# Column strips of 32 at the state products of a state-space layer, and strips by token phase for two of its input units

## The reference, cut to what matters

```python
u, z = proj[..., :1024], proj[..., 1024:]            # proj = h @ w_in
ug = u.reshape(bsz, seq, 64 groups, 16 channels)
in = f * einsum('blgc,gpc->blgp', ug, b)             # complex, 64 states a group
s[t] = a * s[t-1] + in[t]                            # complex scan over tokens
y = real(einsum('blgp,gcp->blgc', s, c)) + d_skip * u
y = gelu(y)
y = y * sigmoid(y @ w_glu + b_glu) * silu(z)
return y @ w_out
```

## Time and profile before

| what | value |
|---|---|
| median of the timed runs | 1353.59 us |
| the profiled execution | 1355.93 us, span 1354.1 us |
| granted TensorE clock, mean | 0.999 |
| PE busy / PE weight loads | 1333.1 us (98%) / 1230.2 us (91%) |
| VectorE busy | 860.0 us (64%) |
| ScalarE busy | 715.9 us (53%) |
| DMA queue for weights | 234.92 MB, 52.6% of 16 engines |

### The profile page before, as it was taken

The page is one execution under the profiler, slowest core; times in us unless marked ns, Lnnn a source line. Parts: engine busy times, 40 slices in busy tenths (PEclk is TensorE's granted clock), DMA queues, the critical chain, the costliest instruction groups (busy, mean ns, idle before and its releaser), DMA issues.

```text
span 1354.1 us, 23214 instructions
## 1 busy us (share of the span) xinstructions
PE 1333.1 (98%) x10110; PEld 1230.2 (91%) x10110; DVE 860.0 (64%) x1003; ACT 715.9 (53%) x954; POOL 54.8 (4%) x70
## 2 busy tenths in 40 slices
PE   6998999999999999999999999999999999999998
PEld 6998889889999989998999998999989999899997
DVE  6999775756555577767645547555466858655553
ACT  5998566655444463375544445444465355544443
POOL 1002000000000003100000000000000500000000
PEclk9999999999999999999999999999999999999999
DMA  9116555455555564455655565556565546555552
GB/s 271 62 32 212 159 199 187 136 179 172 187 190 198 203 205 169 152 190 184 201 187 187 187 208 182 187 190 199 199 205 193 175 133 203 193 187 187 187 187 93
DMA packets 180297, 242.28 MB, mean 179 GB/s; under 512 B 7547, under 2 KB 144005, under 8 KB 180197
## 3 DMA queue, kind: packets, MB, share of 16 engines
q1 hardware_dynamic: 178260, 234.92, 52.6%
q0 software_dynamic: 1648, 5.67, 1.5%
q10 hardware_dynamic: 288, 0.22, 0.0%
HBM read 239.74 MB, written 1.05 MB: 178 GB/s over the span
## 4 chain that ended last, share of the span: by engine, by line
PE 89%; DVE 9%; issue 1%; DMA 1%; ACT 0%; DVEq 0%; ACTq 0%; POOLq 0%
PE P L415 87%; PE P L450 1%; DVE QQ L1761 1%; DMA G<-in_norm_g 1%; DVE YG L1740 0%; DVE WB L1751 0%; DVE QQ L1765 0%; DVE WL L1445 0%; DVE TMPC L1712 0%; DVE TMPC L1709 0%; DVE QQ L1752 0%; DVE X L1725 0%; DVE TMPD L1678 0%; DVE TMPD L1710 0%; DVE DB L1969 0%
## 5 line engine op out<-in xcount | busy, mean ns | idle before, releaser
L1445 DVE TENSOR_TENSOR WL<-RAW,WH 128x2048 fp32r<-128x2048 f32 x214 | 485.7, 2277 | 305.9 <-ACT WH L1013 304.7
L415 PE MATMUL P<-RH,WH 128*128 128x256 f32 x1856 | 516.8, 278 | 4.3 <-DVE RL L1448 3.0
L415 PE MATMUL P<-RL,WH 128*128 128x256 f32 x1856 | 513.8, 277 | 0.0
L415 PE MATMUL P<-RH,WL 128*128 128x256 f32 x1856 | 513.7, 277 | 0.0
L1013 ACT ACTIVATE WH<-RAW 128x2048 fp32r<-128x2048 f32 x214 | 406.4, 1903 | 194.1 <-DMA RAW<-in_ffn_w_down 82.5
L415 PEld LDWEIGHTS P<-RH,WH 128*128 128x128 f32 x1856 | 348.9, 188 | 6.8 <-DVE RL L1448 2.3
L415 PEld LDWEIGHTS P<-RL,WH 128*128 128x128 f32 x1856 | 348.6, 188 | 1.5
L415 PEld LDWEIGHTS P<-RH,WL 128*128 128x128 f32 x1856 | 348.9, 188 | 0.0
L415 PE MATMUL P<-WH,HLO 128*128 128x512 f32 x352 | 138.7, 394 | 0.0
L415 PE MATMUL P<-WL,HHI 128*128 128x512 f32 x352 | 138.1, 392 | 0.0
L415 PE MATMUL P<-WH,HHI 128*128 128x512 f32 x352 | 137.1, 389 | 0.0
(11 more groups left out here) (306 smaller groups left out, 1376.7 us busy)
## 6 DMA issues: line engine op xcount, KB each, us to landing
RAW<-in_ffn_w_gate SPq DMA_DIRECT2D x88, 512.0 KB, 4.3
RAW<-in_ffn_w_up SPq DMA_DIRECT2D x88, 512.0 KB, 5.7
RAW<-in_ffn_w_down SPq DMA_DIRECT2D x44, 1024.0 KB, 5.0
RAW<-in_w_in SPq DMA_DIRECT2D x36, 1024.0 KB, 5.2
RAW<-in_attn_w_in SPq DMA_DIRECT2D x16, 1024.0 KB, 5.3
RAW<-in_ssm_w_in SPq DMA_DIRECT2D x8, 1024.0 KB, 9.6
RAW<-in_w_out SPq DMA_DIRECT2D x8, 1024.0 KB, 5.1
RAW<-in_ssm_w_glu SPq DMA_DIRECT2D x4, 1024.0 KB, 6.9
```

The lines of the kernel that those rows point to most:

```text
L415: return nc.tensor.matmul(*a, **k)
L1445: V.tensor_tensor(WL[:, s, 0:width], RAW[:, s, 0:width], WH[:, s, 0:width].bitcast(f32), SUB).then_inc(sem["lo_split"], 1)
```

## The change

- Units 2 and 3 are no longer multiplied by `plain` but by the new `phased`: for each of the 8 blocks of 32 weight columns, each of 8 contraction tiles and each of 4 phases q one call with 32 stationary columns and 64 moving columns, every fourth token of `XN`, into partitions 32 q to 32 q + 31. The bank then has the layout of X4, and one copy of 128x512 replaces sixteen, on ScalarE for unit 2 and on VectorE for unit 3.
- `states_in` makes each call through `strips`: four calls with 32 stationary columns each, to the four 32-partition parts of the output, with the same moving tile.
- `states_out` goes over half band, phase i and q with strips of 32 columns (one phase of one j each), so that the output's partitions are channels and its columns are phase and chunk. The lifts on VectorE go, and `y_out` is one gelu of 128x512 per band, whose destination steps by four elements.
- ScalarE's split of unit 9 is now made ahead of the last band's gelu, not in the middle of it.

```diff
-LIFT = [4, 4, 2, 2]
+            def phased(u, bank):
+                w = RAW[:, slot_of(u), :].rearrange("p (k c) -> p k c", k=KT)
+                x = XN.rearrange("p k (c i) -> p k i c", i=CL)
+                eng.wait_ge(sem[loaded[slot_of(u)]], pe.next(loaded[slot_of(u)], 16))
+                free(bank)
+                for j in range(8):
+                    for k in range(KT):
+                        for q in range(4):
+                            last = mm(P[bank][32 * q:32 * q + 32, j * NCH:j * NCH + NCH], w[:, k, 32 * j:32 * j + 32],
+                                      x[:, k, CL - 1 - q, :], start=j == 0 and k == 0, stop=j == 7 and k == KT - 1, skip_group_check=True)
+                last.then_inc(sem["unit_used"], 1)
-                plain(cb, cb)
+                (plain if cb == 1 else phased)(cb, cb)
+            def strips(o, lh, rh):
+                for q in range(0, 128, 32):
+                    last = mm(o[q:q + 32], lh[:, q:q + 32], rh, start=True, stop=True, skip_group_check=True)
+                return last
-                        last = mm(PP[2 + b % 2][...], BT[:, ri, j, :], X4[:, j, :], start=True, stop=True)
+                        last = strips(PP[2 + b % 2][...], BT[:, ri, j, :], X4[:, j, :])
-                for jj in range(JB):
-                    j = JB * b + jj
-                    mm(own(jj), TZ[:, j, :], X4[:, j, :], start=jj == 0, stop=False, skip_group_check=True)
+                def own(m, q, i):
+                    c = m * T + i * NCH
+                    return P[Y_BANK[b]][32 * q:32 * q + 32, c:c + NCH]
+                for m in range(2):
+                    for i in range(CL):
+                        for q in range(4):
+                            j = JB * b + 4 * m + q
+                            mm(own(m, q, i), TZ[:, j, 32 * i:32 * i + 32], X4[:, j, :],
+                               start=m == 0 and i == 0, stop=False, skip_group_check=True)
-                        v = CP[:, ri, j, :, :].rearrange("p n c -> p (n c)")
-                        last = mm(own(jj), v, u[:, ri, jj, :], start=False, stop=ri == 1 and jj == JB - 1, skip_group_check=True)
+                for m in range(2):
+                    for i in range(CL):
+                        for ri in range(2):
+                            for q in range(4):
+                                jj = 4 * m + q
+                                last = mm(own(m, q, i), CP[:, ri, JB * b + jj, i, :], u[:, ri, jj, :], start=False,
+                                          stop=m == 1 and i == CL - 1 and ri == 1, skip_group_check=True)
-            for q in range(4):
-                for s in range(CL):
...
+            fn(X4[:, 16:24, :], P[2].rearrange("p (j c) -> p j c", c=NCH), ACT.Copy).then_inc(sem["x4_there_b"], 1)
...
+            V.tensor_copy(X4[:, 24:32, :], P[3].rearrange("p (j c) -> p j c", c=NCH)).then_inc(sem["x4_there_v"], 1)
...
+                dst = YG[:, 2 * b:2 * b + 2, :].rearrange("p m (c i) -> p m i c", i=CL)
+                src = P[Y_BANK[b]].rearrange("p (m i c) -> p m i c", m=2, i=CL)
+                fn(dst, src, ACT.Gelu_apprx_tanh).then_inc(sem["y_raw"], 1)
...
             for b in range(NB):
-                y_out(b, split_hi if b == NB - 1 else None)
+                if b == NB - 1:
+                    split_hi()
+                y_out(b)
                 y_high(b)
...
-            lift(NB - 2)
             split_lo()
             for b in range(NB):
-                if b == NB - 1:
-                    lift(b)
```

More of the change, by code:

```diff
@@ L264, in build @@
             q_made angle_in sines_there f_there small_there b_there cx_there b_turned c_turned bt_there c_there k_there lags_there lags_copied lags_full compact_there ub_cleared tz_there tz_cleared
-            frac_there table_there in_there in_read unrotated y_raw powers_there x4_there_a x4_there_b x4_there_v gain_d_there params_there c_powers b_summed c_summed c_spread y_lifted dec_cleared dec_there scanned x_again
+            frac_there table_there in_there in_read unrotated y_raw powers_there x4_there_a x4_there_b x4_there_v gain_d_there params_there c_powers b_summed c_summed c_spread dec_cleared dec_there scanned x_again
             glu_sig y_gated y_hi y_lo r_hi r_lo qk_squared qk_rms qk_scaled qk_roped qk_turned qk_there gains_in rope_there
@@ L570, in states_in @@
                         j = JB * b + jj
-                        last = mm(PP[2 + b % 2][:, ri * 512 + jj * NCH:ri * 512 + jj * NCH + NCH], BT[:, ri, j, :], X4[:, j, :],
-                                  start=True, stop=True)
+                        last = strips(PP[2 + b % 2][:, ri * 512 + jj * NCH:ri * 512 + jj * NCH + NCH], BT[:, ri, j, :], X4[:, j, :])
                 last.then_inc(sem["in_there"], 1)
@@ L584, in states_out @@
                 u = (UBA, UBB)[b // 2][:, b % 2]
-                def own(jj):
-                    return P[Y_BANK[b]][:, jj * NCH:jj * NCH + NCH]
-                for jj in range(JB):
-                    j = JB * b + jj
-                    mm(own(jj), TZ[:, j, :], X4[:, j, :], start=jj == 0, stop=False, skip_group_check=True)
+                def own(m, q, i):
[7 more added lines that the diff above has]
+                               start=m == 0 and i == 0, stop=False, skip_group_check=True)
                 if b == 0:
@@ L594, in states_out @@
                 eng.wait_ge(sem["unrotated"], b + 1)
-                for jj in range(JB):
-                    j = JB * b + jj
-                    for ri in range(2):
-                        v = CP[:, ri, j, :, :].rearrange("p n c -> p (n c)")
-                        last = mm(own(jj), v, u[:, ri, jj, :], start=False, stop=ri == 1 and jj == JB - 1, skip_group_check=True)
+                for m in range(2):
[5 more added lines that the diff above has]
+                                          stop=m == 1 and i == CL - 1 and ri == 1, skip_group_check=True)
                 last.then_inc(sem["y_summed"], 1)
@@ L1102, in _ @@
             eng.wait_ge(sem["unit_used"], 3)
-            for q in range(4):
-                for s in range(CL):
-                    dst = X4[32 * s:32 * s + 32].rearrange("p (m q) c -> p q m c", q=4)[:, q, 4:6, :]
-                    src = P[2][32 * q:32 * q + 32, :].rearrange("p (m c i) -> p i m c", m=2, i=CL)[:, CL - 1 - s]
-                    fn(dst, src, ACT.Copy).then_inc(sem["x4_there_b"] if q == 3 and s == CL - 1 else act.raised(), 1)
+            fn(X4[:, 16:24, :], P[2].rearrange("p (j c) -> p j c", c=NCH), ACT.Copy).then_inc(sem["x4_there_b"], 1)
             eng.wait_ge(sem["c_turned"], 1)
@@ L1158, in toeplitz, with y_out @@
                            ACT.Copy).then_inc(sem["tz_there"] if lag == CL - 1 else act.raised(), 1)
-            def y_out(b, between=None):
+            def y_out(b):
                 eng.wait_ge(sem["y_summed"], b + 1)
[L1163 to L1175, removed]
+                dst = YG[:, 2 * b:2 * b + 2, :].rearrange("p m (c i) -> p m i c", i=CL)
+                src = P[Y_BANK[b]].rearrange("p (m i c) -> p m i c", m=2, i=CL)
+                fn(dst, src, ACT.Gelu_apprx_tanh).then_inc(sem["y_raw"], 1)
             def y_high(b):
@@ L1731, in lags_back @@
                 V.tensor_copy(KTS[:, 0:4, :], P[2].rearrange("p (m l) -> p m l", m=4)).then_inc(sem["lags_full"], 1)
[L1733 to L1740, removed]
             def rows_of(i, b):
```

## The result

The changed kernel takes 1368.14 us (median of 4, 1367.49 to 1371.27) against 1354.05 us (median of 4 runs of the kernel before): 1.0106 of the time before, 95% interval 1.0094 to 1.0118. That is 14 us slower, where 9 us faster was forecast, and outside the range. The profiled execution took 1367.98 us.

The account below looks back on a forecast made before the run. Three about equally long chains (PE, DVE, ACT) in the first layer's state-space stage bound the gain: second gate unit 10.0 us earlier, less 1.4 for phased units, -8.6 us, median 1345.0 us; range 1340 to 1366.

Parts of the forecast that it names:

- The phased units: Units 2 and 3 on PE: 15 ns a record for stepped reads and instruction stream together, 7.7 us each, +1.4 us in all.
- all three chains: First layer's state-space stage: PE, DVE and ACT work of about equal length, all moved by longer phased units.
- P: Length of one phased unit (2 or 3) on PE; 7.0 us if the step is free, 7.7 taken, upper end 28.
- The formula: Start of the B transposes, and with it all three chains, moves by 2 x (P - 7.0) us.
- Rival 2: Units 2 and 3: the stepped read halves the streams, P = 13.9, net +3.8 us, 1357.4; chance 0.26.
- Rival 4: Instruction fetching, 20 ns a record by the reflection; its own forecast text is not given; counted as same, chance 0.10.
- A strip of 64 columns at 13.6 to 15 ns: State inputs and outputs: 13.6 ns a strip record, 128 records in 1.75 us in place of 3.6; phased units at 15.
- Rotations 3.4 us earlier for the copies removed: DVE: sixteen X4 copies become one, so the first rotation starts at 71.65 in place of 75.05 us.
- One gelu a band at 1.0 us: ACT: the small gelus become four of 128x512, taken at 1.0 us each, bounds 0.6 and 1.6.
- The tail: From PE's last state output at 113.3 us to the second gate unit at 120.6, in place of 120.2 to 130.61.
- The sum without the phased price: Forecast for e1: 10.0 us gain less 3.4 for the returned copies, 6.6 us, about 1347.5.
- rival 5: PE's new idle stretches halve the granted clock for strips and first gate unit, about +3 us; within the forecast's own spread.

Follow-up runs that it names:

- e4: e1 with `plain` reading units 2 and 3's moving operand in phase order, a step of 16 bytes, few records; 1.0089 of the kernel before.
- e2: The changed kernel with `phased` reading 64 neighbouring tokens in place of every fourth one; 1.0127 of the kernel before.
- e5: e1 with the state inputs as full 128-column calls again, strips only at the outputs; 0.9968 of the kernel before.
- e1: The changed kernel with units 2 and 3 back on `plain` and their sixteen small copies back; 0.9971 of the kernel before, 1352.6 us.
- e6: e5 with the loads of units 10 and 11 issued ahead of unit 9's; 0.9984 of the kernel before.
- e11: e5 with the second half of unit 7 ahead of state output 2 in place of between outputs 2 and 3; 0.9977 of the kernel before.

## Why the prediction was wrong, step by step

- **The phased units, the step that failed.** "7.7 us per unit, nearest to the rows for strips as such" measured 16.8 and 15.2 us, +18.0 us on all three chains by the sum of (P - 7.0), where +1.4 was put. The formula held (B transposes +18.7). Rival 2 had the mechanism and nearly the rate, P = 13.9 by 27 ns where e4 gives 14.5, and the twofold of the rows on DVE's stepped copies was there to be read the earlier trace rows, though their sources differ in step too; I set it aside for a port that gives a line per column, which no row showed. Rival 4 put fetching at 20 ns a record, which no row showed; it is 28. Either would have made 14 us or more of a unit. I treated them as two risks that add to a base, and took for "both together" 15 ns, below the 20 and the 27 of each.
- **Fetching at the states, not in the sum.** I named it for `phased` alone. Output 2's stop of 4.25 us and the lowered clock behind it make the last output end 7.5 us after the last rotation, not 1.9. e2, with P near 16 too, has the same 4.27.
- **A strip of 64 columns at 13.6 to 15 ns**: right, 15 ns in short bursts. The 25 ns between starts of the Trainium skill ("TensorE: Matmul & The Clock Gate", section "Wait — 56ns, not 53.3ns?") does not hold for these strips on four positions. But at the state inputs the shorter time was worth nothing (e5 against e1).
- **Rotations 3.4 us earlier for the copies removed**: they gained 18.7 - 15.7 = 3.0 against the shift of the B transposes. Right.
- **One gelu a band at 1.0 us**: 1.06 to 1.15. **The tail**: forecast 7.3 us from the last output to the second gate unit, measured 7.4 (138.0 to 145.4), before 10.4. Right; this 3 us is most of e1's gain of 4.
- **The sum without the phased price** (-6.6 for e1) measured -4.1: of the missing 2.5 us, 1.4 are the stop at output 3 in e1's profile; the rest is within the intervals and not resolved.
- **Clock**: rival 5 was right in kind, from idle times of its size, though behind fetch stops and not behind rotation 3.

## What to carry to other kernels

Four narrow matmuls run side by side, 15 ns a strip of 64 columns where a full record takes 112, but each is an instruction pair of its own: count pairs, not columns. In a long stretch of strips reckon 28 ns a pair, more beside weight loads; a stop came after as few as 122 strips in a row (e5, output 2), elsewhere only after 217 (e1). A float32 moving operand that steps by two elements costs 4%, one that steps by four the double. Where two unknowns bear on the same step, price each by its nearest row and take the larger, not a value for both that no row supports.

## What the runs showed of the hardware that I had not expected

- Instruction pairs of PE come in chunks of 128; one takes about 3.6 us from fetch to fetch when the queues are free (1.0 us of it transfer). Of the 58 stops the 31 with less than 30 GB/s on the other queues from 2.5 us before them to their end are 0.2 to 2.0 us long, the 20 with over 200 GB/s 1.3 to 4.5. That a packet waits behind weight packets fits this and e6, but was not shown. The first burst of e1 got through 217 strips before its first stop. With the borders shifted by 48 records the kernel was about 0.2% faster.
- The same stop can leave the clock or not: after 1.51 us in e5's profile the next group took 3.79 us, after 1.53 us in e11's 6.45 us, with a granted clock of 1.00 and 0.75 from 90 to 100 us. It may be why e11's runs spread so far; that was not tested.
- A moving stream of float32 takes 219 ns per 256 columns contiguous, about 227 at a step of 8 bytes, 453 at 16.
